# A float32 decoder block on one core: the running sums of stick-breaking attention as two fp32r passes, its masks in fewer matmuls, and the final norm's product moved to POOL

## The reference, cut to what matters

```python
def first_block(...):
    ...
    h = h + conv_ffn(...)
    return rmsnorm(h, final_norm_g)

def stick_breaking_attention(q, k, v):        # 8 heads of width 64, strictly causal
    ...
        z = q @ k^T * scale
        log_beta = log_sigmoid(z)
        log_one_minus = where(mask, log_sigmoid(-z), 0)
        tail = cumsum(log_one_minus, reverse over s) - log_one_minus
        weights = where(mask, exp(log_beta + tail), 0)
        out = weights @ v

def second_block(x, ...):
    h = rms_norm(x); q, k, v, glu_a, glu_b = split(h @ w_in)
    q, k = rms_norm per head
    attn = stick_breaking_attention(q, k, v)
    c = silu(layer_norm(causal_depthwise_conv(glu_a * sigmoid(glu_b), 31 taps)))
    x = x + concat(attn, c) @ w_out
    ...                                       # gated FFN
```

## Time and profile before

| | |
|---|---|
| median of 3 runs | 1236.39 us (1236.01 to 1237.41) |
| the profiled execution | 1236.73 us, its span 1235.0 us |
| PE busy | 1223.8 us (99%), 5598 matmuls |
| DVE busy | 601.2 us (49%) |
| ACT busy | 505.1 us (41%) |
| POOL busy | 574.2 us (46%) |
| granted TensorE clock | 1.00 over the span |
| L1562, all heads, share of the chain that ended last | 1% |

### The profile page before, as it was taken

How to read it: one execution, slowest core, us unless ns; L and a number is a source line. 1 busy time by engine, 2 the same in 40 slices (tenths; PEclk the granted TensorE clock), 3 DMA queues, 4 the chain that set the end, 5 groups by cost and what they waited for, 6 DMA issues and landing times.

```text
span 1235.0 us, 16489 instructions
## 1 busy us (share of the span) xinstructions
PE 1223.8 (99%) x5598; PEld 1004.6 (81%) x5598; DVE 601.2 (49%) x877; ACT 505.1 (41%) x674; POOL 574.2 (46%) x465
## 2 busy tenths in 40 slices
PE   9999999999999999999999999999999999999998
PEld 7888888888888888888888886768888888888887
DVE  6782435434653166414575879785334213321431
ACT  7532543343443144313473237666333223332331
POOL 5775553233445344453465441134454444444444
PEclk9999999999999999999999999999999999999999
DMA  8343332112333322232133321102232323223222
GB/s 298 124 145 126 118 103 69 51 69 68 102 102 104 102 85 93 94 119 84 64 124 104 101 86 51 35 18 85 71 104 98 117 88 102 86 85 120 81 76 81
DMA packets 34034, 118.41 MB, mean 96 GB/s; under 512 B 4032, under 2 KB 4160, under 8 KB 33856
## 3 DMA queue, kind: packets, MB, share of 16 engines
q1 hardware_dynamic: 33696, 117.49, 28.6%
q10 hardware_dynamic: 288, 0.24, 0.1%
HBM read 115.61 MB, written 2.10 MB: 95 GB/s over the span
## 4 chain that ended last, share of the span: by engine, by line
PE 95%; ACT 2%; DVE 1%; POOL 1%; issue 1%; DMA 0%; SPq 0%; POOLq 0%; ACTq 0%; DVEq 0%
PE ps L1240 29%; PE ps L1241 29%; PE ps L1242 29%; PE ps L1562 1%; PE ps L1407 1%; PE ps L1545 1%; PE ps L1298 1%; PE ps L1297 1%; PE ps L1296 1%; PE ps L1518 0%; PE ps L1306 0%; POOL w_lo L363 0%; PE ps L1603 0%; ACT slab L654 0%; POOL squares L431 0%
## 5 line engine op out<-in xcount | busy, mean ns | idle before, releaser
L363 POOL TENSOR_TENSOR w_lo<-w_raw,w_hi 128x512 fp32r<-128x512 f32 x430 | 555.3, 1315 | 621.8 <-ACT w_hi L464 355.7
L1240 PE MATMUL ps<-xg_hi,w_hi 128*128 128x512 f32 x960 | 375.7, 391 | 0.0
L1242 PE MATMUL ps<-xg_hi,w_lo 128*128 128x512 f32 x960 | 373.7, 389 | 0.0
L1241 PE MATMUL ps<-xg_lo,w_hi 128*128 128x512 f32 x960 | 373.6, 389 | 0.0
L1240 PE MATMUL ps<-y_hi,w_hi 128*128 128x512 f32 (+1 forms) x608 | 230.8, 380 | 0.0
L1241 PE MATMUL ps<-y_lo,w_hi 128*128 128x512 f32 (+1 forms) x608 | 229.8, 378 | 0.0
L1242 PE MATMUL ps<-y_hi,w_lo 128*128 128x512 f32 (+1 forms) x608 | 229.8, 378 | 0.0
L1240 PEld LDWEIGHTS ps<-xg_hi,w_hi 128*128 128x128 f32 x960 | 180.3, 188 | 37.8 <-issue 0.8
L1242 PEld LDWEIGHTS ps<-xg_hi,w_lo 128*128 128x128 f32 x960 | 180.2, 188 | 37.5
L1241 PEld LDWEIGHTS ps<-xg_lo,w_hi 128*128 128x128 f32 x960 | 180.3, 188 | 37.3 <-issue 0.5
L464 ACT ACTIVATE w_hi<-w_raw 128x1024 fp32r<-128x1024 f32 x124 | 130.5, 1053 | 126.0 <-PE ps L1242 126.0
(11 more groups left out here) (210 smaller groups left out, 1058.1 us busy)
## 6 DMA issues: line engine op xcount, KB each, us to landing
w_raw<-weights SPq DMA_DIRECT2D x199, 512.0 KB, 3.3
w_raw<-weights SPq DMA_DIRECT2D x16, 384.0 KB, 2.9
out_t<-h SPq DMA_DIRECT2D x8, 256.0 KB, 2.1
h<-x_t SPq DMA_DIRECT2D x3, 512.0 KB, 8.4
slab<-mem_t SPq DMA_DIRECT2D x2, 512.0 KB, 10.1
slab<-mats_in SPq DMA_DIRECT2D x1, 1024.0 KB, 7.3
w_raw<-weights SPq DMA_DIRECT2D x2, 256.0 KB, 3.9
h<-x_t SPq DMA_DIRECT2D x2, 256.0 KB, 4.4
```

What stands on the lines that cost most here:

```text
L363: nc.gpsimd.tensor_tensor(w_lo[:, s, half], w_raw[:, s, half], w_hi[:, s, half].bitcast(F32), ALU.subtract).then_inc(done, 1)
L1240: pe.matmul(out, w[0], x[0], start=first, stop=False)
L1241: pe.matmul(out, w[0], x[1], start=False, stop=False)
L1242: return pe.matmul(out, w[1], x[0], start=False, stop=last)
```

## The change

- The stick is split by DVE: a CAST rounds it to fp32r into `stick_hi` (free parts of `y_hi` for even heads, `y_lo` for odd ones), and a subtraction writes the residue over the stick's own memory, seen as fp32r. Both cover all 1280 columns. The three additions into `later_sums` go.
- `s_cumulate` multiplies `neg_tri_r` and `neg_ones_r` (rounded copies, made once early on) with every tile and every later tile directly: ten matmuls on the rounded part, then the same ten on the residue. PE waits for `s_hi` before the first ten, for `s_lo` before the others.
- The masks of tiles 1 and 3, which share a bank, are added by one matmul of 2x128 columns: three per head in place of four.
- The final norm's eight products leave DVE. POOL multiplies `h` by `final_bc`, two tiles after each of the `w_lo` of the blocks QK+4 to QK+7; the gain is multiplied in DVE's residual of the last norm, which was an addition and is now a `scalar_tensor_tensor`.

```diff
-        slab = sb("slab", [P, 28 * SEQ])
+        with nc.sbuf_tensor("slab", [P, 28 * SEQ], F32) as slab:
+            pass
+        slab_r = sb("slab_r", [P, 28 * SEQ], F32R)
...
+        def stick_hi(hd):
+            return (y_hi, y_lo)[hd % 2][:, 4:8, :].rearrange("p a t -> p (a t)")[:, 0:STICK]
+        def stick_lo(hd):
+            return stick_slab_lo[:, hd % 4, :] if hd % 4 < 3 else stick_last_lo
...
-            weights_lo_for(GLU, WOUT2 - GLU)
+            weights_lo_for(GLU, QK + 4 - GLU)
+            pool.wait_ge(spread_copied, NORM_FINAL + 1)
+            for b in range(QK + 4, WOUT2):
+                weights_lo_next(b)
+                for m in (2 * (b - QK - 4), 2 * (b - QK - 4) + 1):
+                    nc.gpsimd.tensor_tensor(h[:, m, :], h[:, m, :], final_bc[:], ALU.mult).then_inc(final_done, 1)
...
+                    if norm == NORM_TWO:
+                        nc.vector.scalar_tensor_tensor(out=new, in0=h[:, m, :], scalar=col("final_norm_g", m), in1=new,
+                                                       op0=ALU.mult, op1=ALU.add).then_inc(summed, 1)
...
-                nc.vector.scalar_tensor_tensor(out=h[:, m, :], in0=h[:, m, :], scalar=col("final_norm_g", m),
-                                               in1=final_bc[:], op0=ALU.mult, op1=ALU.mult).then_inc(final_done, 1)
...
                     nc.vector.tensor_tensor(t[:, c], z_of(hd)[:, c], t[:, c], ALU.max).then_inc(s_stick, 1)
-                    for dst, x, y in ((later[:, 0:P], ...), (later[:, P:2 * P], ...)):
-                        nc.vector.tensor_tensor(dst, x, y, ALU.add).then_inc(vstep, 1)
-                    nc.vector.tensor_tensor(later[:, 2 * P:3 * P], ..., later[:, 0:P], ALU.add).then_inc(s_later, 1)
+                    nc.vector.tensor_copy(hi[:, c], t[:, c]).then_inc(s_hi, 1)
+                    dve.wait_ge(s_hi, n + 1)
+                    nc.vector.tensor_tensor(lo[:, c], t[:, c], hi[:, c].bitcast(F32), ALU.subtract).then_inc(s_lo, 1)
...
-                    for tile in (0, 1, 3, 2):
-                        mm = pe.matmul(ps[:, 3 * (hd % 2) + bank, at:at + P], ident_r[:], far_below_r[:], ...)
+                    pe.matmul(ps[:, bank, 0:P], ident_r[:], far_below_r[:], ...)
+                    pe.matmul(ps[:, bank + 1, :].rearrange("p (a t) -> p a t", t=P)[:, 0:4:3, :], ident_r[:],
+                              far_below_r[:].rearrange("p (a t) -> p a t", a=1).broadcast_to([P, 2, P]), ...)
+                    pe.matmul(ps[:, bank + 2, 0:P], ident_r[:], far_below_r[:], ...)
...
+                def sums_into(tile, stick):
+                    mm = pe.matmul(ps[:, bank, at:at + n], neg_tri_r[:], stick[:, AT[tile]:AT[tile] + n], ...)
+                    for later in range(tile + 1, ST):
+                        mm = pe.matmul(ps[:, bank, at + (later - tile) * P:...], neg_ones_r[:], stick[:, AT[later]:...], ...)
+                    ready(s_hi, 0)
+                    for group in tiles:
+                        for tile in group:
+                            sums_into(tile, stick_hi(hd))
+                    ready(s_lo, 0)
+                    for group in tiles:
+                        for tile in group:
+                            mm = sums_into(tile, stick_lo(hd))
+                        mm.then_inc(s_cum, 1)
```

More of the change, by code:

```diff
@@ L224, in build @@
         neg_ones = sb("neg_ones", [P, P])
-        squares = sb("squares", [P, 5 * SEQ])
+        with nc.sbuf_tensor("squares", [P, 5 * SEQ], F32) as squares:
+            pass
+        squares_r = sb("squares_r", [P, 5 * SEQ], F32R)
         stick_last = squares[:, 2 * SEQ:2 * SEQ + STICK]
+        stick_last_lo = squares_r[:, 2 * SEQ:2 * SEQ + STICK]
         sq = squares[:, 0:2 * SEQ].rearrange("p (a t) -> p a t", t=SEQ)
         ssq = squares[:, 2 * SEQ:4 * SEQ].rearrange("p (a t) -> p a t", t=SEQ)
-        later_sums = sb("later_sums", [P, 2, 3 * P])
+        neg_tri_r = sb("neg_tri_r", [P, P], F32R)
+        neg_ones_r = sb("neg_ones_r", [P, P], F32R)
         rstd_bc = sb("rstd_bc", [P, SEQ])
@@ L1218, in _ @@
             ln_centre()
-            final_norm(range(DT))
             assert not tap_order
@@ L1537, in pair_scores @@
                     pe.wait_ge(banks_freed, QK - USE_LAG)
-                    pe.wait_ge(rounded, 2)
+                    pe.wait_ge(rounded, 4)
                 for tile in (0, 1, 3, 2):
@@ L1547, in pair_scores @@
                 for hd in heads:
-                    for tile in (0, 1, 3, 2):
[L1549 to L1552, removed]
-            def s_cumulate(hd):
[L1556 to L1578, removed]
-                        diagonal(tile)
-                    add(2, P, P, neg_ones, t[:, AT[3]:AT[3] + P])
-                    add(1, P, P, neg_ones, t[:, AT[2]:AT[2] + P])
-                    pe.wait_ge(s_later, hd + 1)
-                    add(1, 2 * P, P, neg_ones, later[:, 0:P]).then_inc(s_cum, 1)
-                if hd == SPLIT_HEAD:
-                    other_tiles()
-                    first_tile()
-                else:
-                    first_tile()
-                    other_tiles()
@@ new lines, in s_cumulate, with ready @@
+            def s_cumulate(hd):
+                parts = log_parts(hd)
+                def ready(done, tile):
+                    c = slice(0, STICK) if len(parts) == 1 else (FIRST if tile == 0 else REST)
+                    pe.wait_ge(done, log_parts_ahead(hd) + parts.index(c) + 1)
+                def sums_into(tile, stick):
+                    bank, at, n = TILES[tile]
+                    bank += 3 * (hd % 2)
+                    mm = pe.matmul(ps[:, bank, at:at + n], neg_tri_r[:], stick[:, AT[tile]:AT[tile] + n], start=False, stop=True,
+                                   skip_group_check=True)
+                    for later in range(tile + 1, ST):
+                        n = TILES[later][2]
+                        mm = pe.matmul(ps[:, bank, at + (later - tile) * P:at + (later - tile) * P + n], neg_ones_r[:],
+                                       stick[:, AT[later]:AT[later] + n], start=False, stop=True, skip_group_check=True)
+                    return mm
+                tiles = ((0,), (1, 2, 3)) if hd != SPLIT_HEAD else ((1, 2, 3), (0,))
+                if hd != SPLIT_HEAD:
+                    ready(s_hi, 0)
[7 more added lines that the diff above has]
+                        mm.then_inc(s_cum, 1)
+                else:
+                    for group in tiles:
+                        ready(s_hi, group[0])
+                        for tile in group:
+                            sums_into(tile, stick_hi(hd))
+                        ready(s_lo, group[0])
+                        for tile in group:
+                            mm = sums_into(tile, stick_lo(hd))
+                        mm.then_inc(s_cum, 1)
```

34 lines of the change are left out of this document (16 added, 18 removed).

## The result

| | before | changed |
|---|---|---|
| median | 1236.82 us (1236.01 to 1237.41, 4 runs) | 1245.12 us (1244.54 to 1246.44, 4 runs) |
| the profiled execution | 1236.73 us | 1245.29 us |
| its span | 1235.0 us | 1243.6 us |

The changed kernel is slower: the ratio is 1.0069, its 95% interval 1.0052 to 1.0086. The forecast was 1245.5 us. The experiments will show that its mechanism held in this kernel, and where two of its terms, and its view of the clock, were off.

The account below looks back on a forecast made before the run. PE (95% of the chain) and DVE were both taken as close to binding, with DVE's lateness deciding: 1236.7 + 9.0 = 1245.7 us, given as 1245.5 because the profiled execution was 0.3 above the median; range 1236 to 1250.5.

Parts of the forecast that it names:

- What bounds, and the sum: Attention stage: about 20 us of added DVE work against 14 us of slack, so DVE's lateness decides, +9.0 us.
- The steps of the last pair: Pair 3: twelve taps end at 820.9, PE waits over 5 us for head 6's CAST, second channel sum 9.0 late.
- the walk: Following the attention stage's four pairs with the estimated durations, to a second channel sum 9.0 us late.
- Turns with POOL: Attention stage: DVE instructions with SBUF inputs and POOL's exclude each other; a POOL instruction costs DVE about 1.1 us.
- The first rival: POOL's products fall in holes and don't take turns with DVE's taps: +2.2 us, 1238.7, partly so up to 1241; chance 0.16.
- their removal is worth nothing to PE: Behind the last head: taking the final norm's products, 8.2 us, off DVE gains PE nothing; its own work hid them.
- `pair_scores(1)`: Pair 0: PE saves 2.4 us of waits and 1.4 of work, loses as much to the new wait; start unchanged, 762.6.
- The clock rival: PE's clock halves after idling over 5 us before head 6: up to 4 us more, 1247 to 1250; chance 0.10.
- PE's saving: Running sums save PE 0.58 us per head, 5.6 us with masks; the rival that this wins had chance 0.10.

Follow-up runs that it names:

- The CAST twice: Changed kernel with the final norm's products late on POOL, each head's CAST issued a second time behind the first: 1247.94 us, ratio 1.0092.
- the filled kernel: Changed kernel with matmuls by zero weights in PE's gaps around head 0's passes and before head 6's sums: 1246.58 us, ratio 1.0079.
- products late: Changed kernel with the final norm's eight products still on POOL, but behind the convolution's second channel sum: 1239.6 us, ratio 1.0027.
- on DVE: Changed kernel with the final norm's eight products back on DVE behind head 7, sums and masks staying changed: 1239.6 us, ratio 1.0029.
- three split heads and the products early: Changed kernel with only heads 2, 3 and 5 split, POOL's products at the changed kernel's places: 1239.54 us, ratio 1.0024.
- three heads of eight: Changed kernel with only heads 2, 3 and 5 split, products late on POOL: 1234.2 us, ratio 0.9981 to the kernel before.
- the kernel with halved products: Changed kernel with POOL's eight products cut into sixteen of 256 columns: 1244.36 us, ratio 1.0064.

## Why the prediction was right, and where it wasn't

*What bounds, and the sum.* The prediction set DVE's 20 us of added work against its 14 us of slack and let DVE's lateness decide. The CAST twice shows it (7 us of added instructions, 7.5 us more of DVE's time, 8.3 us longer), the traced execution of the filled kernel shows that PE's pace doesn't matter in this kernel, and the table that the first charge on the slack was free and the next was not. Predicted +9.0 us in the stage; its length grew by 8.2, and the profiled execution by 8.6.

*The steps of the last pair* came as the walk had them: twelve taps of 11.12 us, over at 821.2 (11 and 820.9 predicted); CASTs of 0.83 us (0.82); PE's wait before head 6 4.7 us (over 5); a pass 1.39 us (1.45).

*Turns with POOL.* Taps of 1.7 us each stand beside POOL's work (two in 3.40 us at 781.28), two products add 2.1 us to seven taps, and a product takes 1.68. The first rival, that they don't take turns, is wrong in the kernel before as well: the seven taps are held up there by the same 2.1 us. The products cost nothing there because DVE had waits (1.03 us before `qk_apply(4)`, 1.77 before head 4) that took in its lateness and that the split uses up.

*Two sizes that were off.* The walk had 2.3 us for the split alone and 6.7 for the products. By the medians they are 3.0 (with the masks' gain in it) and 5.5; by the lengths of the stage 2.4 or 2.9 (products late, or on DVE) and 5.8 or 5.2. The first difference is within the scatter, the second points the same way in both measures, though the medians alone wouldn't show it. The step behind part of it is the prediction's "their removal is worth nothing to PE": ahead of the second channel sum PE waited 0.7 us for additions of POOL that DVE's products held up, and this is what removing them gave. The same walk, made for the products in the kernel before, expected +1.8, and -0.6 came out; the removal explains 0.7 of these 2.4 us, and the rest was not separated. That the total came within 0.4 us is thus partly luck; the mechanism is not.

*`pair_scores(1)`* was predicted to start as before, at 762.6, and started at 764.10, or 763.7 after taking off that this execution entered the stage 0.4 us later. The clock, which fell at 755.5 and held the sums of heads 0 and 1 at half speed, makes 0.8 of these 1.1 us, as the filled kernel shows. The clock rival had it fall only before head 6. This lateness was absorbed before pair 2.

*The clock rival* was half right: the clock fell where it said (0.60 and 0.50 from 820 to 826). Its price, up to 4 us, was wrong for this kernel: the length of the stage with and without the fall is the same. It is not nothing everywhere: where PE's sums were what DVE waited for, the fall cost 1.7 us, with the CAST twice and with three split heads and the products early.

*PE's saving* is real, 0.47 us per head, where DVE has time: heads 2, 3 and 5.

## What to carry to other kernels

Before work is added to an engine that is nearly bound, list its idle pieces where they stand: an addition that falls into them is free, and the next one costs in full, so an edit that costs nothing alone (-0.6 us) can be dear beside another (+5.5). Look also at what the wait does to the engine that has to wait: where PE's clock falls behind it, the price can be more than the lateness. Where two engines hold each other up, ask first where the second's work stands, and move it to a stretch where the first one waits. A part of a change can pay where the whole doesn't: here, three heads of eight.

## What the runs showed of the hardware that was not expected

The granted clock didn't follow PE's idle pieces alone. In the changed kernel PE waited 0.92 and 0.89 us around head 0's first pass and ran at half speed from 755.5 to about 762. In the kernel with halved products it waited 0.93 and 0.88 us at the same places, and 1.25 and 0.89 us more around head 1's first pass, and the clock stayed at 1.00:

```profile
755.00:758.00 3.00, 1.61 (x10) 1.43 (x10) 2.96 (x4) 1.88 (x3) 0.13 (x1) 1.00 0.50 175
758.00:762.00 4.00, 2.71 (x18) 2.48 (x18) 3.97 (x4) 2.25 (x5) 4.00 (x3) 1.00 0.00 0
```

What made the difference wasn't tried. The Trainium skill (TensorE: Matmul & The Clock Gate, "HAM oscillation") lets an engine that was left idle start the next burst at half rate: after the 4.69 us before head 6 the trace agrees (0.50 in the window from 823 on), and of the gaps of 0.9 us one kernel shows it and the other doesn't. A kernel that is marginal in this way may come out with or without the fall.

When DVE and POOL alternate, neither loses the same: two POOL instructions of 512 columns went from 2.53 to 3.37 us beside taps and to 4.1 us beside a subtraction of 1280 columns, while that subtraction went from 1.49 to 2.44. So the long DVE instruction delayed POOL by about its own length (1.56 us for 1.49), and DVE lost 0.95 us to a POOL instruction that takes 1.27 undisturbed.
